# Running sums of a pair of heads: products with the ones matrix of both heads ahead of those with the triangle of both

## What is computed

```python
z = einsum('bhqd,bhkd->bhqk', qx, kx) * scale
causal = s[None, :] < t[:, None]
sp = where(causal, softplus(z), 0.0)
log_rest = cumsum(sp, axis=3, reverse=True) - sp
a = where(causal, exp(log_sigmoid(z) - log_rest), 0.0)
outs.append(einsum('bhqk,bhkd->bhqd', a, vx))
```

## Time and profile before

| | |
|---|---|
| median of 3 runs | 413.68 us (413.5 to 413.97) |
| the profiled execution's own time | 414.61 us |
| its span | 412.8 us |
| TensorE products, weight loads busy | 403.2 us, 371.7 us |
| VectorE, ScalarE busy | 333.6 us, 250.0 us |
| mean granted TensorE clock | 0.995 of full speed |

### The profile page before, as it was taken

The page is one execution under the profiler, slowest core; times in us unless marked ns, Lnnn a source line. Parts: engine busy times, 40 slices in busy tenths (PEclk is TensorE's granted clock), DMA queues, the critical chain, the costliest instruction groups (busy, mean ns, idle before and its releaser), DMA issues.

```text
span 412.8 us, 7093 instructions
## 1 busy us (share of the span) xinstructions
PE 403.2 (98%) x2857; PEld 371.7 (90%) x2857; DVE 333.6 (81%) x441; ACT 250.0 (61%) x295; POOL 28.5 (7%) x40
## 2 busy tenths in 40 slices
PE   8999999999999999999999999999999999999992
PEld 8999988999999999889988899999999999999981
DVE  4689556967765737874858888999999999999986
ACT  6664337864665634551556648777777777777753
POOL 0059400000000000000200000000000000000003
PEclk9999999999999999999999999999999999999997
DMA  8999564534325255555453245555655566555002
GB/s 282 420 421 398 213 203 137 181 125 173 110 101 198 103 205 204 199 183 175 157 176 131 102 143 194 201 199 206 209 207 198 204 213 203 202 203 222 2 0 102
DMA packets 12107, 77.47 MB, mean 188 GB/s; under 512 B 1328, under 2 KB 1328, under 8 KB 3632
## 3 DMA queue, kind: packets, MB, share of 16 engines
q1 hardware_dynamic: 12080, 77.09, 51.6%
HBM read 76.04 MB, written 1.05 MB: 187 GB/s over the span
## 4 chain that ended last, share of the span: by engine, by line
PE 52%; DVE 22%; issue 17%; ACT 3%; DMA 3%; SPq 1%; DVEq 0%; POOL 0%; POOLq 0%; ACTq 0%
PE bank L1154 17%; PE bank L1179 16%; PE bank L1299 11%; DVE w_lo L707 5%; DVE t_lo L707 5%; DVE t_sum L950 4%; DMA raw<-in_weights_dram 3%; DVE t_sum L957 3%; PE bank L1311 1%; DVE forms L1014 1%; DVE res L1087 1%; SPq L332 1%; DVE forms L1024 1%; DVE forms L1019 1%; PE bank L1404 1%
## 5 line engine op out<-in xcount | busy, mean ns | idle before, releaser
L707 DVE TENSOR_TENSOR w_lo<-raw,w_hi 128x2048 fp32r<-128x2048 f32 (+2 forms) x83 | 145.3, 1756 | 26.4 <-ACT w_hi L455 25.2
L1154 PE MATMUL bank<-hT_hi,w_hi 128*128 128x256 f32 x386 | 107.0, 278 | 0.6 <-DVE hT_lo L719 0.4
L1154 PE MATMUL bank<-hT_lo,w_hi 128*128 128x256 f32 x384 | 106.3, 277 | 0.0
L1154 PE MATMUL bank<-hT_hi,w_lo 128*128 128x256 f32 x384 | 106.2, 277 | 0.0
L455 ACT ACTIVATE w_hi<-raw 128x2048 fp32r<-128x2048 f32 x33 | 62.9, 1916 | 29.4 <-PE bank L1154 13.9
L1154 PEld LDWEIGHTS bank<-hT_hi,w_hi 128*128 128x128 f32 x386 | 72.4, 188 | 1.1 <-issue 0.6
L1154 PEld LDWEIGHTS bank<-hT_lo,w_hi 128*128 128x128 f32 x384 | 72.3, 188 | 0.1
L1154 PEld LDWEIGHTS bank<-hT_hi,w_lo 128*128 128x128 f32 x384 | 72.1, 188 | 0.0
L707 DVE TENSOR_TENSOR t_lo<-t_sum,t_hi 128x1024 fp32r<-128x1024 f32 x30 | 36.5, 1218 | 0.0
L1299 PE MATMUL bank<-hT_hi,w_hi 128*128 128x256 f32 x128 | 35.8, 279 | 0.0
L1299 PE MATMUL bank<-hT_lo,w_hi 128*128 128x256 f32 x128 | 35.4, 277 | 0.0
(11 more groups left out here) (206 smaller groups left out, 856.1 us busy)
## 6 DMA issues: line engine op xcount, KB each, us to landing
raw<-in_weights_dram SPq DMA_DIRECT2D x65, 1024.0 KB, 4.8
head_all<-in_triples_dram SPq DMA_DIRECT2D x6, 384.0 KB, 6.5
raw<-in_chunk_dram SPq DMA_DIRECT2D x2, 512.0 KB, 8.2
res<-in_x_dram SPq DMA_DIRECT2D x2, 512.0 KB, 13.0
mem_tok<-in_mem_dram SPq DMA_DIRECT2D x1, 1024.0 KB, 13.0
memT_raw<-in_memT_dram SPq DMA_DIRECT2D x1, 1024.0 KB, 11.2
out_dram<-xs SPq DMA_DIRECT2D x2, 512.0 KB, 2.6
gfin<-in_g_final_dram SPq DMA_DIRECT2D x1, 512.0 KB, 5.6
```

The source lines that it names most:

```text
L707: return nc.vector.tensor_tensor(dst, whole, high.bitcast(fp32), sub)
L1154: last = mm(outs[m][:, tok], w, v[:, k0 + k, tok], start=first and n == 0 and not t, stop=k == nk - 1 and n == 2, skip_group_check=bool(kt ...
```

## The change

Within each pair, the two products with `neg_ones_r` of both heads are issued first (4 products), then the two with `neg_tri_r` of both heads (4 products). The products, their operands, their number, the wait ahead of them and the signal behind the last of them stay. Within one head, and so within one bank, the order stays as well.

```diff
                 pe.wait_ge(sp_lo_done, p + 1)
                 for i in range(2):
-                    z = bank[SB_Z[i]]
                     for sp in (sp_hi, sp_lo):
-                        mm(z[:, 128:256], neg_ones_r[:, :], sp[:, i, 256:384], start=False, stop=False,
+                        mm(bank[SB_Z[i]][:, 128:256], neg_ones_r[:, :], sp[:, i, 256:384], start=False, stop=False,
                            skip_group_check=True)
-                    mm(z[:, 0:384], neg_tri_r[:, :], sp_hi[:, i, :], start=False, stop=False, skip_group_check=True)
-                    last = mm(z[:, 0:384], neg_tri_r[:, :], sp_lo[:, i, :], start=False, stop=True,
-                              skip_group_check=True)
+                for i in range(2):
+                    for sp in (sp_hi, sp_lo):
+                        last = mm(bank[SB_Z[i]][:, 0:384], neg_tri_r[:, :], sp[:, i, :], start=False,
+                                  stop=sp is sp_lo, skip_group_check=True)
                 last.then_inc(sb_c, 1)
```

## The result

| | before | changed |
|---|---|---|
| median of 6 runs | 413.59 us (413.07 to 413.97) | 415.34 us (414.9 to 415.67) |
| ratio, 95% interval | | 1.0035 (1.002 to 1.005) |
| span of the profiled execution | 412.8 us | 413.9 us |

The changed kernel is slower by 0.35%, with an interval that leaves no room for "no change". The prediction was wrong: it had 413.7 us, a range up to 414.4 and 5% for slower by over 0.2%.

The account below looks back on a forecast made before the run. TensorE was taken as the bound, busy throughout at full clock. Terms of 0 + 0 + 0 for each of four pairs left the median at 413.7 us, range 413.0 to 414.4, with 0.91 for within 0.2%.

Parts of the forecast that it names:

- What bounds the kernel: From 96 to 128 us TensorE is busy throughout at full clock, so its queue's gains or losses go to the end.
- What a product costs: In the sums, the longer of load and stream: 110 ns for a ones product, 174 ns for a triangle product.
- the sum for a pair: Eight products of the sums: 4 x 110 + 4 x 174 = 1,136 ns, as before; difference 0.
- The eight starts: Products of a changed pair start at 0, 0.06, 0.17, 0.28, 0.39, 0.62, 0.79 and 0.96 us.
- The repeated weights: In the sums, four products in a row with the same weights spare no load; value 0, at most 0.64 us.
- the banks: Two more bank changes in each pair's sums, eight in all, cost 0; upper bound 0.08 us.
- who waits behind: ScalarE's exponential behind the sums has 2.9 us of slack, so a delay there would be hidden.
- No load was spared: Rival in the sums: equal weights in a run spare loads, 413.0 to 412.8 us; chance 0.03.
- a price on bank changes: Rival: eight additional changes between banks 4 and 5 cost up to 0.88 us, 413.7 to 414.6 us; chance 0.04.
- the last rival: Mixed order let loads run ahead under long products; grouping loses up to 0.85 us, 414.5 us; chance 0.03.
- Ones products in a row: Rival: four short products in the sums run faster than a load, 0.42 us in all, 413.3 us; chance 0.02.
- There are three things that could cost or give something: Loads, repeated weights and banks in the sums are the only possible effects of the new order, each 0.

Follow-up runs that it names:

- e9: Kernel before with the sums' lengths in the old order but a change of bank at every product, seven in a pair; ratio 1.0002 (0.9993 to 1.0011).
- e6: Kernel before, sums in the old order, one product in the middle of the last half gate column split into two of 128 columns; ratio 1.0025 (1.0009 to 1.004).
- e3: Kernel before with only the sums of the last pair (pair 3) in the new order; ratio 1.0025 (1.0014 to 1.0037).
- e12: Kernel before with each pair's sums ordered short, short, short, long, short, long, long, long; ratio 1.0045 (1.0028 to 1.0063).

## Why the prediction was wrong

- *What bounds the kernel.* Right: TensorE is busy throughout, and all that its queue loses between 80 and 170 us goes to the end.
- *What a product costs, and the sum for a pair.* Right inside the block: 1.15 us in both kernels, for the 1.14 forecast. The eight starts came as said within 0.02 us.
- *The repeated weights, the banks, who waits behind.* Right. All loads are there, bank changes cost nothing (e9), and nobody waits longer.
- *The rivals.* None took place. No load was spared, and the slower one I gave most room, a price on bank changes, was refuted. The mixed order hid 0.004 us a pair more than the grouped one, not the 0.2 us of the last rival. Ones products in a row start 0.11 us apart (111.84, 111.95, 112.07); the Trainium skill (TensorE: Matmul & The Clock Gate, "Back-to-back issue gap") has about 81 ns for that size in a sustained stream, and this trace does not agree, four in a row as little as two.
- *The step that failed* is "There are three things that could cost or give something": loads, repeated weights and banks, all inside the eight products, by the rule that "every product still adds the longer of load and stream, whoever its neighbours are". The sum has no term for the products of 256 columns behind them (L1299 and the branch's 240), and so takes for granted that they cost what they cost before. They don't: they run at 113.3 or 117.8 ns, by the state that the products ahead leave. That term was left at 0 without a reason, and measured 0.24 + 0.04 - 0.09 + 1.06 = 1.25 us. The last sentence of the prediction named the finding, an unchanged block and another time at the end, and said that I had no mechanism.
- *It could have been read.* The chain of the kernel before has the same 24 products once with 2.75 and once with 3.02 us, and I stopped at the block. With that row there would have been a rival on the slower side: the 240 products at the other pace, 240 x 4.5 ns = 1.1 us, which is close to what came. Its sign could have been read too, since the branch was in the faster of the two paces and could only lose. Whether the new order would turn the pace could not.

How the 1.27 us of the traces stand to the medians: 1.27 of 413.59 is a ratio of 1.0031, inside both intervals for this kernel (1.002 to 1.005 and 1.0026 to 1.0056). The medians differ by 1.75 and 1.55 us; the rest isn't assigned to any stretch.

No version here beats the kernel before. In both profiles of it the slow pace lies in the last half gate column, in 24 products of the cross-attention's queries, and in 119 products from 8.7 us on. These last are fast in the first profile of the changed kernel, and the 217 products of the queries and keys start no earlier for it (26.59 us, against 26.80 and 26.43), so no gain is seen there. In the other two the pace is worth some 0.1 us each. Breaking it costs a load of 0.11 us each time, and in the last half gate column, as e6 shows, it turns the branch slow. What could be won is under 0.2 us by this estimate, less than the intervals here can show, so it wasn't tried.

## What to carry to other kernels

When a change reorders a few products on a saturated TensorE, cost not only them but ask what the long uniform stretch behind them will do: compare the time per product of equal groups in the chain of waits, and look whether the trace shows more than one. If a stretch runs slow for no visible reason (no wait, full clock, every product a few ns longer), split one product inside it into two short ones and look again; here that took 0.84 us from a stretch of 28.5. Look again in more than one profile, since a split right behind a wait or another kind of product was followed by the slow pace twice in 28 cases. Judge an order of products by the whole stage, since a gain or loss of this kind comes with orders that are equal by every other account.

## What the runs showed of the hardware that I had not expected

- Two stable paces for the same 256-column float32r product with its load, 113.3 and 117.8 ns, at a granted clock of 1.00, each kept over 200 products and more. What makes them is not shown, nor whether it lies in TensorE itself. In the fast one all loads are recorded with 187 to 188 ns, in the slow one every third with 192.
- The pace is handed on in turned form. In all 14 profiles of this study, a last half gate column that ends fast is followed, behind 16 products of attention (L1311), by a branch that starts slow, and one that ends slow by a fast one. Between 80 and 170 us the pattern was the same in both profiled executions of each of the two kernels.
- Where a stretch starts from a wait for other engines, the pace does vary. The 217 products of the queries and keys, which no kernel here touches, were fast in 12 of the 14 profiles and slow in those of e3 and e12. In e12 the slow pace began only at 28.59 us, behind a product that was held up for 0.1 us. The chain's row of e3, for a stretch that takes 24.61 us in the kernel before:

```profile
26.63 25.55 PE bank L1154 x217
```

- That is 0.94 us in one execution, with nothing in the kernel to account for it, which is why a single profile of this kernel can't decide a difference of 0.3%, while its rows can say in which stretch it lies.
